# Rows of the norm parameters spread by TensorE and ScalarE instead of five broadcast loads, in a two-layer RWKV/mLSTM/attention/PEER kernel

## The reference, cut to what matters

```
for layer in range(2):
    mixer = even_mixer if layer == 0 else odd_mixer
    x = layer_norm(ALPHA * x + mixer(x), ln1_g, ln1_b)
    x = layer_norm(ALPHA * x + peer_ffn(x), ln2_g, ln2_b)
```

## Time and profile before

| | |
|---|---|
| device time of 3 runs | 1779.08, 1779.93, 1780.38 us |
| the profiled execution | 1780.13 us, span 1777.7 us |
| PE busy | 1538.4 us (87%), 6020 records |
| DVE busy | 1062.2 us (60%) |
| ACT busy | 604.7 us (34%) |
| POOL busy | 576.6 us (32%) |
| gathered rows (queue q0) | 73728 packets, 536.90 MB |
| loads and stores (queue q1) | 18240 packets, 100.24 MB |
| all DMA | 638.32 MB, mean 359 GB/s |
| chain that ended last | PE 52%, DMA 34%, ACT 6%, DVE 6% |

### The profile page before, as it was taken

How to read it: one execution, slowest core, us unless ns; L and a number is a source line. 1 busy time by engine, 2 the same in 40 slices (tenths; PEclk the granted TensorE clock), 3 DMA queues, 4 the chain that set the end, 5 groups by cost and what they waited for, 6 DMA issues and landing times.

```text
span 1777.7 us, 18617 instructions
## 1 busy us (share of the span) xinstructions
PE 1538.4 (87%) x6020; PEld 921.1 (52%) x6020; DVE 1062.2 (60%) x2499; ACT 604.7 (34%) x1759; POOL 576.6 (32%) x561
## 2 busy tenths in 40 slices
PE   8999988999877778998899978998999968777776
PEld 7779977764322225763456525663457523222222
DVE  1584634577888875334556447665556468874444
ACT  1434411233333333227532323346632323332222
POOL 2000000244444442233432442334432444443441
PEclk9999958999999999999999999999999999999999
DMA  6222003899999999999999999999999999999996
GB/s 250 96 74 93 1 1 111 342 411 427 426 427 427 426 427 422 427 426 427 427 424 425 421 427 425 427 426 427 427 382 426 397 426 427 427 427 427 427 427 275
DMA packets 92063, 638.32 MB, mean 359 GB/s; under 512 B 11072, under 2 KB 13120, under 8 KB 15424
## 3 DMA queue, kind: packets, MB, share of 16 engines
q0 software_dynamic: 73728, 536.90, 71.8%
q1 hardware_dynamic: 18240, 100.24, 14.4%
HBM read 636.05 MB, written 1.05 MB: 358 GB/s over the span
## 4 chain that ended last, share of the span: by engine, by line
PE 52%; DMA 34%; ACT 6%; DVE 6%; issue 3%; POOL 1%; ACTq 0%; SPq 0%; POOLq 0%; DVEq 0%
DMA arena<-l_peer_uv,arena 33%; PE psum L905 22%; PE psum L587 14%; PE psum L886 5%; DVE arena L1715 3%; PE psum L764 2%; PE psum L809 1%; PE psum L680 1%; PE psum L670 1%; PE psum L679 1%; ACT L1202 1%; POOL arena L554 1%; ACT arena L1207 1%; ACT early L1215 1%; ACT arena L1215 1%
## 5 line engine op out<-in xcount | busy, mean ns | idle before, releaser
L554 POOL DMA_INDIRECT arena<-l_peer_uv,arena x512 | 563.4, 1100 | 1089.3 <-PE psum L905 828.9
L1715 DVE CUSTOM_DVE_ANT_0 arena<-arena,xres 128x1024 f32<-128x1024 f32 x512 | 619.3, 1223 | 406.5 <-DMA arena<-l_peer_uv,arena 400.9
L905 PE MATMUL psum<-arena,early 128*128 128x512 f32 x1024 | 477.6, 611 | 99.8 <-ACT early L1215 96.4
L905 PE MATMUL psum<-arena 128*128 128x512 f32 x1024 | 474.5, 608 | 95.7 <-ACT arena L1215 92.2
L905 PEld LDWEIGHTS psum<-arena,early 128*128 128x128 f32 x1024 | 189.4, 193 | 359.5 <-issue 200.4
L905 PEld LDWEIGHTS psum<-arena 128*128 128x128 f32 x1024 | 189.1, 192 | 354.8 <-issue 210.4
L587 PE MATMUL psum<-xT,wring 128*128 128x128 f32 (+2 forms) x1856 | 295.9, 319 | 12.5 <-DMA wring<-l_w_in 8.2
L587 PEld LDWEIGHTS psum<-xT,wring 128*128 128x128 f32 (+1 forms) x1856 | 268.5, 191 | 51.6 <-issue 21.1
L1202 ACT ACTIVATE arena<-arena 128x2 f32<-128x2 f32 x256 | 52.0, 203 | 595.4 <-DVE arena L1715 595.1
L1030 ACT COPY arena<-psum 128x256 f32<-128x256 f32 (+2 forms) x138 | 62.5, 472 | 220.8 <-PE psum L587 117.3
L1207 ACT ACTIVATE arena<-arena 128x1 f32<-128x1 f32 x512 | 123.3, 287 | 23.8
(11 more groups left out here) (236 smaller groups left out, 1142.7 us busy)
## 6 DMA issues: line engine op xcount, KB each, us to landing
wring<-l_w_in SPq DMA_DIRECT2D x47, 1024.0 KB
wring<-l_peer_wq SPq DMA_DIRECT2D x24, 1024.0 KB
wring<-l_w_out SPq DMA_DIRECT2D x12, 1024.0 KB
arena<-l_peer_uv,arena POOLq DMA_INDIRECT x512
ln_par<-l_ln_g SPq DMA_DIRECT2D x6, 512.0 KB
ln_par<-l_ln_b SPq DMA_DIRECT2D x6, 512.0 KB
arena<-l_peer_keys SPq DMA_DIRECT2D x2, 1024.0 KB, 6.9
xT<-x_t SPq DMA_DIRECT2D x1, 1024.0 KB, 4.8
```

What stands on the lines that cost most here:

```text
L554: pool.indirect_dma_start(out=ring[:, g % RING, :], out_offset=None, in_=T[f"l{l}_peer_uv"], in_offset=bass.IndirectOffsetOnAxis(ap=eid[:, ...
L905: last = mm(self.ps[c], diag[k % DIAGS], ring[:, g % RING, D + c * 512:D + (c + 1) * 512], start=not self.begun, stop=True, skip_group_che ...
L1715: v.tensor_tensor_reduce(out=u, in0=u, in1=xres[:, self.b, :], scale=1.0, scalar=0.0, op0=ALU.mult, op1=ALU.add, accum_out=hid[:, self.b, ...
```

## The change

Six rows (g and b of layer 0 norm 2, layer 1 norm 1, layer 1 norm 2) are laid into one array of 6 x 1024 and loaded once, 24 KB, into partitions 0 to 5 of the tile `masks`, which the first mixer has finished with by then. Before each of the five norms that need new parameters, PE copies two of the rows to all partitions: four calls of 128 x 512 (`spread_ln`) whose stationary operand is one column of the identity, repeated 128 times over 6 partitions. ACT copies the four banks into `ln_par` (`take_ln`). DVE waits for ACT's copies in place of the load. The first parameters are still broadcast at the start.

```diff
+    plan += [("ln_row", 4)]
     for b in range(NB):
-        plan += [..., ("fox_rms", 4)]
+        plan += [..., ("fox_rms", 4), ("ln_row", 4)]
         plan += [(name, 1) for name, _ in attention_plan(b)]
         plan += [("o_turn", 2), ("mix_out", 2), ("x_turn", 2)] + [("peer_q", 1), ("peer_s", 1)] * GROUPS
+        plan += [("ln_row", 4)]
...
-            load_ln(0)
+            sp.dma_start(ln_par[:, 0, :], T["l0_ln1_g"].partition_broadcast(P)).then_inc(S("ln_loaded"), 16)
+            sp.dma_start(ln_par[:, 1, :], T["l0_ln1_b"].partition_broadcast(P)).then_inc(S("ln_loaded"), 16)
             load_strips(16 + WRING - 3)
             await_filled(sp, "seq_y", NCH - 1)
             load_keys(0)
+            sp.dma_start(ln_rows, T["ln_rows"]).then_inc(S("ln_rows_loaded"), 16)
             load_strips(6 - WRING)
-            load_ln(2)
             load_strips(6)
...
             for b in range(NB):
                 load_strips(17 - WRING * (b == 0))
-                load_ln(3 + 2 * b)
                 load_strips(4 + 8)
-                load_ln(4 + 2 * b)
...
+            def spread_ln(i):
+                pe.wait_ge(S("ln_rows_loaded"), 16)
+                for t in range(4):
+                    r, c = 2 * LN_ROWS[i] + t // 2, t % 2
+                    done(mm(claim(pe, "ln_row", 4 * i + t), ident[0:6, r:r + 1].to_broadcast([6, P]),
+                            ln_rows[:, c * 512:(c + 1) * 512], start=True, stop=True), "ln_row")
...
+            def take_ln(i):
+                act.wait_ge(S("x_normed"), i + 2)
+                for t in range(4):
+                    taken(copy(ln_par[:, t // 2, t % 2 * 512:(t % 2 + 1) * 512], full(act, "ln_row", 4 * i + t)), "ln_row")
...
-                dve.wait_ge(S("ln_loaded"), 32 * NORM_LOADS[e])
+                if NORM_LOADS[e] == 1:
+                    dve.wait_ge(S("ln_loaded"), 32)
+                else:
+                    dve.wait_ge(S("ln_row_taken"), 4 * (NORM_LOADS[e] - 1))
```

More of the change, by code:

```diff
@@ L179 @@
 NORMS = [(0, 0), (0, 1), (1, 0), (2, 0), (1, 1), (2, 1), (3, 0), (3, 1)]
+LN_ROWS = [NORMS[e][0] - 1 for e in range(2, len(NORMS) - 1)]
 NORM_LOADS = [sum(NORMS[i][0] != NORMS[i - 1][0] for i in range(1, e + 1)) + 1 for e in range(len(NORMS))]
@@ L201, in bank_plan @@
         plan += [("peer_q", 1)] * (h < EH - 1) + [("peer_s", 1)]
+    plan += [("ln_row", 4)]
     for b in range(NB):
-        plan += [("experts", 2), ("x_turn", 2), ("fox_f", 1), ("fox_qk", 4), ("fox_v", 2), ("fox_og", 2), ("fox_rms", 4)]
+        plan += [("experts", 2), ("x_turn", 2), ("fox_f", 1), ("fox_qk", 4), ("fox_v", 2), ("fox_og", 2), ("fox_rms", 4),
+                 ("ln_row", 4)]
         plan += [(name, 1) for name, _ in attention_plan(b)]
         plan += [("o_turn", 2), ("mix_out", 2), ("x_turn", 2)] + [("peer_q", 1), ("peer_s", 1)] * GROUPS
+        plan += [("ln_row", 4)]
     plan += [("experts", 2)]
@@ L288, in build @@
         level_mask = masks[:, 2 * P:8 * P].rearrange("p (g n) -> p g n", g=6)
-        acc = masks[:]
+        ln_rows = masks[0:6, :]
         early = sb("early", [P, 4 * P])
@@ L943, in mixer1 @@
                 ex.pairs(RMS_PAIRS)
+                spread_ln(1 + 2 * b)
                 pe.wait_ge(S("qk_normed"), 4 * (b + 1))
@@ L1009, in _ @@
             ex.pairs(sum(later_pairs(g, i) for g in range(GROUPS) for i in range(8)))
+            spread_ln(0)
             ex.finish()
@@ L1015, in _ @@
                 mixer1_tail(b, ex)
+                spread_ln(2 + 2 * b)
                 ex.finish()
@@ L1287, in mixer1 @@
                 ex.pairs(RMS_PAIRS)
+                take_ln(1 + 2 * b)
                 w = P * (b + 1)
@@ L1337, in _ @@
             gates(1, PAIRS, lambda g, i: ex.pairs(later_pairs(g, i)))
+            take_ln(0)
             ex.finish()
@@ L1344, in _ @@
                 mixer1_tail(b, ex)
+                take_ln(2 + 2 * b)
                 ex.finish()
@@ L1727, in add @@
                     for c in range(2):
-                        part = acc[:, c * 512:(c + 1) * 512]
+                        part = masks[:, c * 512:(c + 1) * 512]
                         row = ring[:, g % RING, D + c * 512:D + (c + 1) * 512]
@@ L1757, in combine @@
                             dve.wait_ge(S(f"half_sums{c}"), rows_before(DVE_ROW, n + 1))
-                            st.then(tt(x, x, acc[:, c * 512:(c + 1) * 512], ALU.add))
+                            st.then(tt(x, x, masks[:, c * 512:(c + 1) * 512], ALU.add))
                         st.settle()
@@ L1882 @@
         laid[f"l{l}_peer_keys"] = keys.reshape(2 * EH, NK, P).transpose(2, 0, 1)
+    laid["ln_rows"] = _np.stack([laid.pop(f"{norm}_{part}") for norm in ("l0_ln2", "l1_ln1", "l1_ln2") for part in "gb"])
     for w in ("l0_w_in", "l0_w_out", "l0_peer_wq", "l1_w_in", "l1_w_out", "l1_peer_wq"):
```

## The result

| | before | after |
|---|---|---|
| median of 9 runs each | 1780.67 us | 1787.23 us |
| lowest to highest | 1779.08 to 1784.70 | 1783.60 to 1791.21 |
| profiled execution, span | 1780.13, 1777.7 us | 1786.78, 1785.0 us |
| granted clock, mean | 0.969 | 0.964 |

The ratio is 1.0033, with a 95% interval of 1.0020 to 1.0046. The change costs 5.9 us (0.33% of 1780 us); forecast was no difference, 1779.8, and the range ended at 1785.0. The forecast is wrong.

What follows compares the result with a forecast made beforehand. DMA bounds the kernel to 1066 us, PE to about 1400, then DMA again. Two loads -4.92, spread 3 +4.2, spread 4 +3.0 and restart queue -2.4 sum to -0.1 us: median 1779.8 us, 8-in-10 range 1773.5 to 1785.

Steps and rivals of the forecast that it cites:

- the first of "what is added": Each spread's four PE calls take 3.44 us, as the same shape does in the trace; using 6 rows gains nothing.
- spread 1: At 822.5 us, ahead of block 0's attention: PE 3.44 us late but DMA stays full; cost 0, without cover 3.4.
- Block 0's loads, -4.92: Loads at 788 and 983 us, where DMA is full: removing them saves 2.46 us each.
- Spread 3, +4.2: At 1214.5 us, on PE's path: 3.44 us plus a wait for ACT's last copy; bounds 3.4 to 5.8.
- Spread 4, +3.0 and -2.4: At 1398.5 us: PE's next pairs come 3.0 us later; 2.4 us is given back by the queue at the gathers' restart.
- L: Time from issue to landing of one gather on an empty DMA: 3.6 to 7.4 us, taken as 5.5; skill's rule 4.4.
- Two further at 4.9 us behind it: Restart near 1400 us: the gather two after the first lands 4.9 us behind it, DMA being full from there.
- Loads of block 1, 0: Loads at 1180 and 1380 us: their bytes are worth 0, since gaps in DMA follow at 1302 and 1396 us.
- Spreads 0 and 2, hidden: Near 645 and 1001.4 us: PE's waits and gathers in flight cover them; cost 0, for the second up to 1.8 us.
- Rival 2: Slower: ring runs dry behind spreads, at 1002 and 1400 us, if L is over 7; 1783.7 to 1785.3 us, chance 0.20.
- Rival 1: DMA sets the time all through, four loads count 9.8 us, PE's additions hide: 1770.3 us; chance 0.20 with its milder form.
- its milder form: The spread at 1214.5 us hides behind other PE waits, such as 7.1 us for ACT: 1775.8 us; within Rival 1's 0.20.

Runs made afterwards that it cites:

- k128: Kernel after, with the spreads' matmuls over 128 rows instead of 6, sums unchanged; 1782.50 us, ratio 1.0008 to the kernel before.
- mixed128: Kernel after with 128-row spreads for block 0 alone, three other parameter pairs loaded as before; 1775.35 us (0.9965), repeated at 1777.64 us (0.9992).
- only4: Kernel before with only the spread ahead of pass 3, 128 rows, four loads kept; 1782.08 us, ratio 1.0015.
- both: Kernel before with its five loads kept and five 6-row spreads added, ACT copying them to an unused place; 1790.64 us, ratio 1.0055.
- no34: Kernel before without the loads of 1180 and 1380 us and without spreads (another function); 1778.29 us, ratio 0.9988.
- neither: Kernel after without spreads and without the five loads, later norms using the first norm's parameters (another function); 1775.44 us, ratio 0.9968 to the kernel before.
- only3: Kernel before with only the spread in front of block 1's attention, 128 rows, four loads kept; 1783.87 us, ratio 1.0021.
- mixed6: Spreads for block 0 alone with 6 rows instead of 128, other three parameter pairs loaded; 1779.74 us, ratio 0.9994 to the kernel before.
- zeros: Kernel after with 128-row spreads, rows beyond the six loaded as zeros in one 512 KB load; 1783.40 us, ratio 1.0020 to the kernel before.

## Why the prediction was wrong, point by point

**The step that failed** is the first of "what is added": "Below I take 3.44 us", and "That only 6 of 128 rows are used I count as no gain: the columns are the same". The duration of one call was right at full clock (587 ns a record in after, 592 with 128 rows). But I took the clock as given. Fewer rows made the granted clock fall to 0.50 in all five places, for the later records of spreads 1, 3 and 4 above all and for the pairs and scores behind all five. Price by the runs: 1.0033 against 1.0011 for the three versions of 128 rows, 3.9 us. That the rows are the cause and that it costs time is shown; the size is known to within 2.6 us. The rows 5 and 6 on which I called spread 1 hidden were read well for a delay of 3.44 us: k128 keeps DMA at 415 GB/s there. They did not cover the delay that it became. From the spread's start at 819.69 to the end of the pair at 830.94 us (825.67 + 5.27) after takes 11.25 us; scores and pair alone take 4.35 at full clock in mixed128 (827.60 to 831.95). So PE was 6.9 us late, twice the forecast. As an estimate from these rows: of the 14.35 us that the gather of 822.75 took, an empty DMA needs 5.8 (only4), which leaves 8.5 to spare; 6.9 and the 2.46 of the missing load are 9.4, 3.44 and 2.46 only 5.9. So the load that is gone had been part of the cover. The DMA rate from 822 to 845 us fits: 426 GB/s before, 409 in both (the loads kept, 6 rows), 415 in k128 and 344 in after. The size of the hole in after, 4.4 us of bytes, is more than this estimate gives.

The Trainium skill, page "TensorE: Matmul & The Clock Gate", section "Why this matters for your kernels", says that a single matmul over 32 rows takes the same time as one over 128. The trace agrees while the clock is at 1.00 (6 rows 587 ns a record, 128 rows 592), but not for four calls, eight records, in a row, where the last records take up to 1056 ns. The same page and section of the Trainium skill tie a fall of the clock to an idle engine; the fall at 1206 us before agrees (4.59 us of waiting), the five behind the spreads don't, since PE had records back to back.

**Block 0's loads, -4.92.** Right: -4.0 to -5.0 us by the marks in the six versions with the clock held and these loads gone, -6.2 and -1.4 by the two sets of runs of mixed128. In after only 2.1 of it was left.

**Spread 3, +4.2.** Right in its parts (3.60 and 0.77 us, "an ACT copy ahead of it") and, as far as can be told, in size: 3.7 by the runs (1.6 to 5.9), 5.8 by the marks. In after the half clock is added: L957 takes 1.23 us instead of 0.70 and the pair 4.32 instead of 3.70.

**Spread 4, +3.0 and -2.4.** The second term is wrong. L was 5.8 for 5.5, which is 0.3; the other 1.5 is that the second row into an empty DMA comes 3.9 us behind the first. "Two further at 4.9 us behind it" took the full rate for rows that are only just being issued, 1.5 to 1.7 us apart. Together +1.8, and only4 measured 2.7 for 0.6. The prediction's other figure for L, 4.4 us, was further off.

**Loads of block 1, 0.** Too low by some 2 us (no34, 0.4 to 3.9).

**Spreads 0 and 2, hidden.** Spread 0 is, even at half clock: 427 GB/s from 636 to 642 us in after. Behind spread 2 DMA is full at first (1.02 from 1003 to 1007 us, where I had named a share under 0.95 as the sign of an error) but comes to 391 GB/s over 1002 to 1020 us, 424 before: 0.6 MB, 1.4 us. In k128 it is 419, 0.2 us.

**Sum with measured terms**: -4.9 (block 0's loads, by the marks) + 3.7 + 2.7 = +1.5 us at full clock; the versions of 128 rows measured +1.1 to +3.6. With 3.9 us for the clock that is +5.4, and the change measured +5.9. By these middle values, of the 6.0 us between forecast and result 3.9 are the clock and 2.1 the restart (what the loads of block 1 save is inside the 3.7 and 2.7); half a us off at spread 3 and half a us left over are below what these runs can tell.

**Rivals.** Rival 2, that the ring runs dry behind the spreads, named the right symptom (DMA share 0.00 at 1408 us), the right sign and nearly the price (to 1785.3), but a wrong cause, since it was to decide at L over 7, and it did not name 822 us, where the most was lost (at 1002 us 1.4 us are missing). Rival 1 is out: neither, with all loads and spreads gone, gains 5.7 us and not 9.8, and its milder form, in which spread 3 hides, does not go with the +3.7 us of only3. No case of mine held what happened. The rows used were the one property of their shape in which the new calls differed from the nearest row (128 there, 6 here), and I gave it no bound on the bad side.

## What to carry to other kernels

Several matmuls in a row that use few rows can cost more than their own time: look at the granted clock behind them, and if it falls, let them run over all 128 rows against zeros of the stationary operand (the other one must hold finite numbers), at 592 ns a record for 587. Replace a load by engine work only in the stage that DMA sets, and keep the load where the engine sets the time: the version that did so (mixed128) was 0.35% and 0.08% faster in two sets of runs (the second not clear of zero), while doing it everywhere was 0.1% slower even at full clock. When you price a delay at the restart of a queue, count the rows until it is full again, not the first alone.

## What the runs showed of the hardware that was not expected

- The granted clock fell from 1.00 to 0.50 while PE had records back to back, with four calls of 6 x 512 as what changed. It was seen in all five places of after, in four of the five of both, and in both of mixed6; with 128 rows in none of the five places of k128 and zeros, whether these rows held mask values or zeros. Whether the rows of the moving or of the stationary operand count, and what 32 or 64 rows would do, was not tried.
- A gather of 1 MB on an empty DMA took 5.8 to 6.1 us from issue to the first use on DVE. In only4 the next came 3.91 us behind it and in after 3.54 (1415.30 and 1418.84), the third 2.45 and 2.43. The next gather was issued 1.5 to 1.7 us behind each time; one alone was not tried.
- The pair behind a spread of 6 rows, itself of 128 rows, ran its 8 records in 5.75 us at 1405 us where 3.60 is usual: work behind pays for the work ahead.
